# Moving the output accumulators, half a projection and GpSimd's first loads in a three-layer transformer kernel

## What is computed

```
mod  = silu(c) @ w_mod + b_mod                      # first block: six vectors of 1024 (and the same for the context)
h    = rms_norm(x) * (1 + mod[1]) + mod[0];  proj = h @ w_in          # tokens and 256 context tokens
mix  = [differential attention (4 heads x 128), gated linear attention (256), neighbourhood attention (256)]
x   += mod[2] * (mix @ w_out)
x   += mod[5] * experts(rms_norm(x) * (1 + mod[4]) + mod[3])          # 32 experts in 4 groups, top 2, hidden 512
x    = rms_norm(x, final_g)

for layer in range(2):                              # second block
    proj = rms_norm(x) @ w_in
    mix  = [latent attention (8 heads x 64), stick-breaking attention (256), pooling mixer (256)]
    x   += mix @ w_out                              # (256 x 1024) @ (1024 x 1024)
    x   += experts(rms_norm(x))                     # 32 experts, top 2, hidden 256
x    = rms_norm(x, final_g_2)
```

## Time and profile before

| stage | from, to (us) | what |
|---|---|---|
| start | 0 to 50 | parameters, four modulation pieces, first norm |
| input projection | 50 to 211 | with modulation pieces 4 to 11 |
| first mixer | 211 to 293 | |
| output projection, norm, routing | 293 to 351 | |
| experts of the first block | 351 to 836 | |
| layer 0: up to the latent attention | 849 to 924 | |
| latent attention | 924 to 948 | |
| output projection, norm, routing | 948 to 1007 | |
| experts | 1007 to 1236 | |
| layer 1, the same | 1242 to 1656 | latent attention at 1317, experts at 1400 |

### The profile page before, as it was taken

How to read it: one execution, slowest core, us unless ns; L and a number is a source line. 1 busy time by engine, 2 the same in 40 slices (tenths; PEclk the granted TensorE clock), 3 DMA queues, 4 the chain that set the end, 5 groups by cost and what they waited for, 6 DMA issues and landing times.

```text
span 1656.4 us, 31626 instructions
## 1 busy us (share of the span) xinstructions
PE 1348.4 (81%) x12376; PEld 714.5 (43%) x12377; DVE 440.6 (27%) x1329; ACT 395.5 (24%) x766; POOL 44.6 (3%) x68
## 2 busy tenths in 40 slices
PE   3899976888767786799968888977889887999875
PEld 2655444354333343355546544433337544443332
DVE  0103356432111111122234513211122524222112
ACT  2101224122111121122223412222132412222222
POOL 3000110000000000000000000000000000000000
PEclk8999978979888898899979889999899997999998
DMA  9968310369999999999764156999993315679994
GB/s 338 347 232 264 106 65 13 142 271 409 410 410 410 410 409 410 410 364 410 281 254 153 55 207 273 417 417 418 418 359 113 118 68 203 273 286 419 417 417 189
DMA packets 126304, 479.77 MB, mean 290 GB/s; under 512 B 9185, under 2 KB 19774, under 8 KB 109550
## 3 DMA queue, kind: packets, MB, share of 16 engines
q1 hardware_dynamic: 122496, 468.61, 72.1%
q0 software_dynamic: 2848, 8.86, 1.8%
q10 hardware_dynamic: 910, 1.59, 0.3%
HBM read 477.05 MB, written 1.97 MB: 289 GB/s over the span
## 4 chain that ended last, share of the span: by engine, by line
PE 53%; SPq 20%; DMA 12%; DVE 8%; issue 4%; ACT 2%; ACTq 0%; POOL 0%; DVEq 0%
SPq L500 20%; DMA store<-in_w_up 9%; PE psum L1041 6%; PE psum L1739 6%; PE psum L717 5%; PE psum L1018 4%; PE psum L1031 4%; PE psum L991 4%; PE psum L1052 3%; PE psum L1735 2%; PE psum L1059 2%; PE psum L1280 2%; PE psum L1292 2%; PE psum L592 2%; PE psum L1325 1%
## 5 line engine op out<-in xcount | busy, mean ns | idle before, releaser
L1031 PE MATMUL psum<-store 128*32 128x256 f32 x2624 | 184.6, 424 | 60.9 <-DMA store<-in_w_expert_up 60.7
L1041 PE MATMUL psum<-store 128*32 128x256 f32 x2432 | 151.4, 404 | 32.4 <-DMA store<-in_w_up 32.0
L1183 DVE TENSOR_TENSOR store<-store,psum 128x128 f32<-128x128 f32 x79 | 22.7, 288 | 536.2 <-ACT store L1116 536.2
L1031 PEld LDWEIGHTS psum<-store 128*32 128x32 f32 x2624 | 80.8, 118 | 145.7 <-DMA store<-in_w_expert_up 91.2
L991 PE MATMUL psum<-xn,store 128*32 128x256 f32 (+1 forms) x992 | 132.4, 503 | 5.4 <-DVE store L1146 5.4
L1018 PE MATMUL psum<-store 32*128 32x256 f32 (+1 forms) x992 | 130.5, 483 | 1.9 <-ACT store L1121 1.9
L1041 PEld LDWEIGHTS psum<-store 128*32 128x32 f32 x2432 | 89.1, 116 | 84.5 <-issue 50.3
L1116 ACT ACT_TABLE_LOAD x79 | 101.4, 1283 | 49.0 <-issue 48.7
L1116 ACT ACTIVATE store<-psum 128x128 f32<-128x128 f32 x79 | 21.9, 278 | 322.6 <-PE psum L1031 188.7
L1739 PE MATMUL psum<-store 128*128 128x512 f32 x224 | 97.7, 593 | 0.0
L1018 PEld LDWEIGHTS psum<-store 32*128 32x128 f32 (+1 forms) x992 | 60.3, 196 | 75.4 <-issue 69.7
(11 more groups left out here) (323 smaller groups left out, 1451.7 us busy)
## 6 DMA issues: line engine op xcount, KB each, us to landing
store<-in_w_expert_up SPq DMA_DIRECT2D x128, 1024.0 KB, 18.3
store<-in_w_expert_down SPq DMA_DIRECT2D x64, 1024.0 KB, 18.4
store<-in_w_gate SPq DMA_DIRECT2D x64, 1024.0 KB, 19.0
store<-in_w_up SPq DMA_DIRECT2D x64, 1024.0 KB, 21.0
store<-in_w_down SPq DMA_DIRECT2D x64, 1024.0 KB, 21.8
store<-in_w_mod SPq DMA_DIRECT2D x12, 2048.0 KB, 14.8
store<-in_w_in SPq DMA_DIRECT2D x6, 2048.0 KB, 10.4
store<-in_w_out SPq DMA_DIRECT2D x6, 2048.0 KB, 14.0
```

The lines of the kernel that those rows point to most:

```text
L1031: mm = pe.matmul(out_(j), chosen_rows(k, 0), wt[:, kk, :, j, :], start=(k == 0), stop=(k == KD - 1))
L1041: mm = pe.matmul(out_(j), chosen_rows(k, e), wt, start=(k == 0), stop=(k == KD - 1))
```

## The change

There are three parts.

1. GpSimd waits for `mod_mm` 4, the fourth modulation product, after its three memsets and before its first load. The waits for `bias_out` on ScalarE and VectorE move from ahead of all units to ahead of the units of piece 2. VectorE's lambda sums move to the units of piece 4.
2. The latent attention uses banks 4 to 7: scores of item i in bank 4 + i % 2 (both heads), transposes in bank 6, values in bank 7 (halves by group, and the wait for a copied-out group is for the one before, in place of two before). Half 1 of the output projection is issued in it, two of 16 matmuls for each item, between `scores(i + 2)` and `turns(i)`. Its slots are released behind the attention. In the first block the halves stay where they were.
3. The experts' accumulators move from banks 4 to 7 to banks 0 to 3, and what was in banks 0 to 3 (logits, ranks, U, Y, G, GT) to 4 to 7. The clearing matmuls move from behind the logits to behind the residual (`clear_pe`), ahead of the norm's transposes, in all three layers.

```diff
+        def score_of(kind, i):
+            if kind == "mla":
+                return ps[4 + i % 2].rearrange("p (m n) -> p m n", m=2)
+            return psum[:, 2 * (i % 2):2 * (i % 2) + 2, :]
+        def turned_of(kind, i, m):
+            if kind == "mla":
+                return ps[6][:, S * m:S * m + S]
+            return ps[4 + (i % 2 if kind == "diff" else m)]
+        def values_of(kind, g):
+            return ps[7][:, S * (g % 2):S * (g % 2) + S] if kind == "mla" else ps[6 + g % 2][:, 0:S]
...
-                if g >= 2:
-                    pe.wait_ge(*at.plus("pv_sb", g - 1))
-                bank = ps[6 + g % 2]
+                lag = 1 if kind == "mla" else 2
+                if g >= lag:
+                    pe.wait_ge(*at.plus("pv_sb", g + 1 - lag))
+                bank = values_of(kind, g)
...
                     scores(i + 2)
+                if fill:
+                    fill(i)
                 turns(i)
...
-        def out_projection_pe(pe, at, piece_ready, kind, mix):
...
+        def out_steps_pe(pe, slot, j, first, last):
+            w = piece_at(slot, 4 * D).rearrange("p (k n) -> p k n", k=4)
+            for step in range(first, last):
+                t, n, k = step // 8, step // 4 % 2, step % 4
+                mm = pe.matmul(ps[2 * t + n], mixT[:, 4 * j + k, P * t:P * t + P], w[:, k, 512 * n:512 * n + 512],
+                               start=(j == 1 and k == 0), stop=(j == 0 and k == 3))
+                if step % 8 == 7:
                     mm.then_inc(sems["out_mm"], 1)
+        def out_free_pe(pe, at):
+            pe.wait_ge(*at("out_mm", 2))
+            pe.sem_inc(sems["piece_used"], 2)
+        def out_rest_pe(pe, at, piece_ready, kind):
+            slot = piece_ready((kind, 0))
+            pe.wait_ge(*at("mixed"))
+            out_steps_pe(pe, slot, 0, 0, 16)
+            out_free_pe(pe, at)
...
+        def clear_pe(pe, at, adds):
+            pe.wait_ge(*at("zero_tile"))
+            pe.wait_ge(*at("resid", adds))
+            for b in range(4):
+                pe.matmul(ps[b], zeros, X[:, 0, 0:512], start=True, stop=True)
...
             mm.then_inc(sems["logits"], 1)
-            pe.wait_ge(*at("zero_tile"))
-            for b in range(4, 8):
-
-                pe.matmul(ps[b], zeros, xn[:, 0, 0:512], start=True, stop=True)
             pe.wait_ge(*at("route"))
...
-        U, Y, G, GT = ps[0], ps[1], ps[2], ps[3]
+        U, Y, G, GT = ps[4], ps[5], ps[6], ps[7]
...
-                attention_pe(pe, at, "mla")
-                out_projection_pe(pe, at, piece_ready, "wout2", mixT)
+                slot = piece_ready(("wout2", 1))
+                attention_pe(pe, at, "mla", fill=lambda i: out_steps_pe(pe, slot, 1, 2 * i, 2 * i + 2))
+                out_free_pe(pe, at)
+                out_rest_pe(pe, at, piece_ready, "wout2")
+                clear_pe(pe, at, 3 * NT if layer == 0 else 2 * NT)
...
             pool.memset(wdec, 0.0).then_inc(sems["zero_done"], 1)
+            pool.wait_ge(sems["mod_mm"], 4)
             pool.dma_start(const1, ins["const1"]).then_inc(sems["params2"], 16)
...
-            act.wait_ge(sems["bias_out"], 16)
             for n, (kind, of, what, i, who) in enumerate(UNITS):
                 if kind != "X" and of != piece:
+                    if of == 2:
+                        act.wait_ge(sems["bias_out"], 16)
...
-            dve.wait_ge(sems["bias_out"], 16)
             for n, (kind, of, what, i, who) in enumerate(UNITS):
                 if kind != "X" and of != piece:
+                    if of == 2:
+                        dve.wait_ge(sems["bias_out"], 16)
                     if 2 <= of <= 5:
                         mod_columns(next(mods))
                         mod_columns(next(mods))
+                    if of == 4:
+                        lambdas()
```

More of the change, by code:

```diff
@@ L540, in keys_of, with attention_pe @@
             return P * (t + 1) if kind == "mla" else 4 * P
-        def attention_pe(pe, at, kind, between=None):
+        def score_of(kind, i):
[8 more added lines that the diff above has]
+            return ps[7][:, S * (g % 2):S * (g % 2) + S] if kind == "mla" else ps[6 + g % 2][:, 0:S]
+        def attention_pe(pe, at, kind, between=None, fill=None):
             items = items_of(kind)
@@ L557, in scores @@
                         q, k = (qnT if kind == "na" else qaT)[r, g, P * t:P * t + P], k_all[r, g, :]
-                    mm = pe.matmul(ps[2 * (i % 2) + m][:, 0:keys_of(kind, t)], q, k, start=True, stop=True)
+                    mm = pe.matmul(score_of(kind, i)[:, m, 0:keys_of(kind, t)], q, k, start=True, stop=True)
                 mm.then_inc(sems["score"], 1)
@@ L568, in turns @@
                 for m in range(1 if kind == "diff" else 2):
-                    bank = ps[4 + (i % 2 if kind == "diff" else m)]
+                    bank = turned_of(kind, i, m)
                     for c in range(keys_of(kind, t) // P):
@@ L704, in attention_dve @@
             at("score", len(items)), at("exps", len(items)), at("pv", len(items) // 2)
-        def out_projection_pe(pe, at, piece_ready, kind, mix):
[L709 to L719, removed]
-                    mm.then_inc(sems["out_mm"], 1)
-                pe.wait_ge(*at("out_mm", 2))
-                pe.sem_inc(sems["piece_used"], 2)
+        def out_steps_pe(pe, slot, j, first, last):
[5 more added lines that the diff above has]
+                if step % 8 == 7:
+                    mm.then_inc(sems["out_mm"], 1)
+        def out_free_pe(pe, at):
[6 more added lines that the diff above has]
+            out_free_pe(pe, at)
         def residual_dve(dve, at, link, bank, done, gate=None, quarters=False):
@@ L906, in extra_rounds_dve @@
         def extra_rounds_dve(dve, at, link, which):
-            r = ps[1][:, 0:3 * NE].rearrange("p (n e) -> p n e", e=NE)
+            r = ps[5][:, 0:3 * NE].rearrange("p (n e) -> p n e", e=NE)
             at_once = experts_of(which)
@@ L1016, in combine @@
                         r = slice(w * n, w * n + w)
-                        out_ = ps[4 + n][:, S * t:S * t + S] if which == 1 else ps[4 + 2 * t + n]
+                        out_ = ps[n][:, S * t:S * t + S] if which == 1 else ps[2 * t + n]
                         mm = pe.matmul(out_, comb[r, P * t:P * t + P], y_sb[r, 0:S * at_once], start=False, stop=True,
@@ L1815, in _ @@
             pe.wait_ge(*at("gla_y"))
-            out_projection_pe(pe, at, piece_ready, "wout", mixT)
+            slot = piece_ready(("wout", 1))
+            out_steps_pe(pe, slot, 1, 0, 16)
+            out_free_pe(pe, at)
+            out_rest_pe(pe, at, piece_ready, "wout")
+            clear_pe(pe, at, NT)
             norm_pe(pe, at)
```

32 lines of the change are left out of this document (17 added, 15 removed).

## The result

The changed kernel takes 1641.1 us (median of 4 runs, 1638.56 to 1642.88), the kernel before 1658.62 beside it (4 runs). The ratio is 0.989, with a 95% interval of 0.9868 to 0.9911: faster by 17.5 us. 1641.6 was forecast. The profiled execution took 1640.6 us, its span is 1638.7 and its mean granted clock 0.919.

The account below looks back on a forecast made before the run. A load was taken to bound the start, then TensorE's chain up to mid-experts, then weight loads. Gains of 5.2 + 13.4 - 1.3 = 17.3 us from 1658.29 gave 1641.0, plus 0.6 for the median: 1641.6 us, range 1632 to 1652.

Parts of the forecast that it names:

- Bounds and shift: Whole kernel: a load bounds the start, then TensorE's chain up to mid-experts; time saved ahead of the experts is kept.
- Part 1: Start: GpSimd's loads no longer delay the fourth modulation piece; 5.2 us gained, bounds 0 and 5.7.
- Part 2: Latent attention: half the output projection fills TensorE's waits; 6.7 us gained a layer, 13.4 for both, bounds 3.5 and 10.
- the 0.4 taken off for a low clock: Latent attention: 0.4 us a layer deducted because the clock may still be down when the first fill runs.
- the 0.3 for the change of piece: Output projection: 0.3 us counted before and after the change for the change of piece up to the second half.
- The bound of 10: Latent attention: at most 10 us gained a layer, if busy rows, whose ends overlap, overstate the work.
- Part 3: Projection to experts, three times: moved clears speed transposes but slow ranks and gather; 1.3 us lost in all.
- Rival B: Logits: clears ahead hold the upper clock through them, 3.5 in place of 7.0 us, three times; 1631 us, chance 0.13.
- C: Latent attention: it keeps its clock dips, so the fill gains only 3.6 us a layer; 1647.8 us, chance 0.15.
- D: Start: GpSimd's wait gives nothing, as modulation pieces are queue-bound or the store comes late; 1646.8 us, chance 0.10.
- E: Latent attention: fills run at 1.2 GHz, 1.75 us each; 31 us slower in sum, 1690 us, chance 0.04.
- The "wrong if" tests: Wrong if attention takes 35 us or more, fourth piece lands after 36, or projection-to-first-up-product changes by over 3 us.

Follow-up runs that it names:

- experiment 1: The kernel before with only GpSimd's wait for the fourth modulation product, and the later scratch-store waits and lambda sums: 1651.02 us against 1658.25, ratio 0.9954.

## Why the prediction was right, and where its terms were off

**Bounds and shift.** As predicted in the main: the load at the start and TensorE's chain to the experts carried the shift, and the weight loads behind moved along with it. Not all of it was "kept to the end": of the lead at the first expert round of each layer, 1.5 us (layer 0) and 1.4 us (layer 1) are gone at the end of the rounds. No run shows why.

**Part 1, forecast 5.2.** Right by a little too small a size: 6.3 us at the first unit, 7.6 by experiment 1. The upper bound of 5.7, GpSimd's share of the DMA engines' time, was 3.0 up to the piece's issue and 2.7 behind it. Measured, the issue moved by 3.1 us (norm_g, which it waits for, landed at 13.03 where it was 16.17), as the share says, and the piece was on its way 3.2 us less. Why that is 0.5 more than the share stays open. That its chain of loads would be hidden held (59.3 us, forecast 60.7).

**Part 2, forecast 6.7 a layer, measured 9.5 and 9.7.** The mechanism held: TensorE is the bound, the inner waits are gone, the waits at the ends are there (1.16, 0.75 and 1.09 us, forecast 2.64 in all). The mis-sized term is TensorE's own work, 3.62 us for two items: it is 2.96 (6.40 less two fills of 1.72). I had added durations of consecutive rows, which overlap. The differences of their starts don't. Four pairs make 2.6 us of it, the longer waits at the ends (3.0 in place of 2.64) take 0.4 back, and the stage comes out at 29.0 in place of 31.1. Beside these 2.1 us, the 0.4 taken off for a low clock wasn't needed, and of the 0.3 for the change of piece nothing is left: 6.7 + 2.1 + 0.4 + 0.3 = 9.5. The bound of 10, given for just this overlap, held.

**Part 3, forecast -1.3, measured -7.5.** This step failed, within its bounds of -4 for each of three. Where the clears would stand, what they would wait for, and that transposes and logits would start sooner was right. Three terms were mis-sized:

- The loss behind the idle time, forecast at 0.6 + 1.0 + 0.3 = 1.9 us, was 5.2 in layer 0: 2.7 from the ranks to the up product (10.25 us against 7.57) and 2.5 in the up product, which the sum left out. What failed is "I estimate the loss at half of what a full halving costs, since a gather is dense enough to end the dip": the gather took 3.68 us, all at the lower level, and the up product behind it 6.21.
- The gain ahead of it, forecast at 1.4, was 4.6 in layer 0: 1.3 at the transposes and 3.3 at the logits, which the sum left at the lower level. So in this stretch the net of -0.7 comes near the forecast -0.5 by two errors that cancel.
- The wait in the first block, forecast at 0.4, was 2.3 us.

And "at the old place the four clears cost nothing" was true but missed what they gave: they kept TensorE busy in the 5 us in which VectorE routes. The 7.5 us are the medians' difference; of them 3 to 5 us can be found beside the clears.

**Rival B** came in partly. The Trainium skill (TensorE: Matmul & The Clock Gate, Part 1) has the clock follow how busy TensorE has been, and by it the logits would stay at the upper level. They ran in 3.73 us in layer 0, 5.11 in the first block and 4.88 in layer 1, against 7.01: by that rule, the trace agrees in one of the three places in full. In layer 0 the gain was lost again behind the idle 5 us, where ranks and gather ran at the lower level; the same rule would have pointed there. Rivals C, D and E are refuted: clock 1.00 in the attention, 5 us and more from the start, fills at 0.86 us each (1.72 for two).

The "wrong if" tests: attention 29.0 (under 35), fourth piece before 32.9 (under 36), projection's end to first up product shorter by 1.9 us in layer 0 (under 3). None fired. The third was set at the wrong place: it ended ahead of the up product, which alone lost 2.55 us.

The terms were 5.2 + 13.4 - 1.3 = 17.3. The experiments make them about 7 + 19.6 - 7.5 = 19, with some us of uncertainty each; measured as a whole 17.5. So the total was right because an underrated fill (6.2 us) and an underrated loss (6.2 us) cancelled: that is luck.

## What to carry to other kernels

A zeroing matmul, or any other work with no hurry, can be worth more in TensorE's idle time just ahead of a critical stretch than out of the way: ask what the clock will be when the wait ends. Here four dense matmuls more in the first block and in each layer, with no use in the result, made the kernel 10 us faster. And ask whether the new place is off the critical path everywhere: in the first block it wasn't. When work is stacked into a stage, add the starts' differences of its rows, not their durations.

## What the runs showed of the hardware

- With 5.0 us without TensorE work ahead of them, the ranks ran at the lower level in all 15 places of five profiles (0.63 to 0.64 us for the first pair) and the gather in all ten of the layers (3.28 to 3.68 us). With four dense matmuls in that time the ranks ran fast in all 15 places of five other profiles (0.30 to 0.41 us), and the gather took 1.94 us in eight of ten (else 2.74 and 3.61). With two of them the gather was slow throughout, and the ranks in one place of three.
- The same logits (16 matmuls of 36 columns) took 3.73 to 6.66 us behind clears and transposes at the upper level, and 4.61 to 7.02 us behind idle time and slow transposes. So where a dip falls differs from one execution to the next.
- GpSimd's 1.55 MB of loads at the start delayed the fourth piece by 6.3 us, more than the 5.7 us of DMA engine time that its queue's shares make.
